# A decoder layer on one core: 18 of the 22 gate and up pairs of each SwiGLU as seven block products of 256 columns

## The reference

```
x = x + 0.5 * swiglu(rms_norm(x, g1), Wg1, Wu1, Wd1)     # d_ff 2816
x = x + mixer(rms_norm(x, g2))                           # pooling and windowed attention
x = x + 0.5 * swiglu(rms_norm(x, g3), Wg2, Wu2, Wd2)
x = x + sigmoid(rms_norm(x, g4) @ Wg) * (p @ Wp)
swiglu(h, Wg, Wu, Wd) = (silu(h @ Wg) * (h @ Wu)) @ Wd
```

## Time and profile before

| | |
|---|---|
| median of 3 runs | 924.93 us |
| profiled execution, first to last instruction (its span) | 923.8 us |
| TensorE busy, matmuls | 918.1 us, 4166 matmuls |
| VectorE / ScalarE / GpSimd busy | 300.1 / 337.4 / 408.1 us |
| granted TensorE clock | full speed throughout |

### The profile page before, as it was taken

How to read it: one execution, slowest core, us unless ns; L and a number is a source line. 1 busy time by engine, 2 the same in 40 slices (tenths; PEclk the granted TensorE clock), 3 DMA queues, 4 the chain that set the end, 5 groups by cost and what they waited for, 6 DMA issues and landing times.

```text
span 923.8 us, 11585 instructions
## 1 busy us (share of the span) xinstructions
PE 918.1 (99%) x4166; PEld 758.7 (82%) x4166; DVE 300.1 (32%) x479; ACT 337.4 (37%) x499; POOL 408.1 (44%) x192
## 2 busy tenths in 40 slices
PE   9999999999999999999999999999999999999998
PEld 8888888888888888887788888888888888888887
DVE  7522121111200501778958621112222200400552
ACT  5633232223321411568844632233322321321451
POOL 0544444444444444256665444444444444444430
PEclk9999999999999999999999999999999999999999
DMA  7633333333223243221224243333333323232211
GB/s 213 176 114 91 94 110 91 91 93 109 93 92 92 90 114 92 69 71 55 70 70 115 75 129 91 91 101 104 91 91 99 105 92 91 95 111 91 92 66 49
DMA packets 131044, 89.28 MB, mean 97 GB/s; under 512 B 11552, under 2 KB 116296, under 8 KB 131016
## 3 DMA queue, kind: packets, MB, share of 16 engines
q1 hardware_dynamic: 131000, 88.90, 32.7%
q10 hardware_dynamic: 16, 0.00, 0.0%
HBM read 86.80 MB, written 2.10 MB: 96 GB/s over the span
## 4 chain that ended last, share of the span: by engine, by line
PE 98%; DVE 1%; ACT 0%; issue 0%; DVEq 0%
PE bank L1282 32%; PE bank L1283 31%; PE bank L1284 31%; PE bank L1297 1%; PE bank L1507 1%; PE bank L1370 0%; DVE pr_lo L1093 0%; PE bank L1406 0%; ACT probs L623 0%; DVE d_lo L1054 0%; DVE probs L1086 0%; DVE probs L1071 0%; PE bank L1462 0%; PE bank L1463 0%; ACT w_hi L450 0%
## 5 line engine op out<-in xcount | busy, mean ns | idle before, releaser
L350 POOL TENSOR_TENSOR w_lo<-raw,w_hi 128x1024 fp32r<-128x1024 f32 x157 | 382.0, 2435 | 473.2 <-ACT w_hi L450 250.0
L1282 PE MATMUL bank<-h_hi,w_hi 128*128 128x512 f32 x844 | 329.9, 391 | 0.0
L1284 PE MATMUL bank<-h_hi,w_lo 128*128 128x512 f32 x844 | 328.6, 389 | 0.0
L1283 PE MATMUL bank<-h_lo,w_hi 128*128 128x512 f32 x844 | 328.5, 389 | 0.0
L1282 PEld LDWEIGHTS bank<-h_hi,w_hi 128*128 128x128 f32 x844 | 158.4, 188 | 33.9 <-issue 0.3
L1284 PEld LDWEIGHTS bank<-h_hi,w_lo 128*128 128x128 f32 x844 | 158.4, 188 | 32.9
L1283 PEld LDWEIGHTS bank<-h_lo,w_hi 128*128 128x128 f32 x844 | 158.5, 188 | 32.5
L508 ACT ACTIVATE w_hi<-raw 128x1024 fp32r<-128x1024 f32 x80 | 84.6, 1060 | 243.3 <-PE bank L1284 243.3
L450 ACT ACTIVATE w_hi<-raw 128x1024 fp32r<-128x1024 f32 x77 | 81.4, 1059 | 221.4 <-PE bank L1284 221.4
L1282 PE MATMUL bank<-act_hi,w_hi 128*128 (+1 forms) x352 | 136.9, 389 | 0.0
L1283 PE MATMUL bank<-act_lo,w_hi 128*128 (+1 forms) x352 | 136.9, 389 | 0.0
(11 more groups left out here) (181 smaller groups left out, 593.8 us busy)
## 6 DMA issues: line engine op xcount, KB each, us to landing
raw<-in_ffn_w_down SPq DMA_DIRECT2D x44, 512.0 KB, 3.7
raw<-in_ffn_w_gate SPq DMA_DIRECT2D x42, 512.0 KB, 3.9
raw<-in_ffn_w_up SPq DMA_DIRECT2D x42, 512.0 KB, 3.9
raw<-in_w_ple_gate SPq DMA_DIRECT2D x8, 512.0 KB, 3.7
raw<-in_w_in SPq DMA_DIRECT2D x6, 512.0 KB, 4.0
raw<-in_w_in SPq DMA_DIRECT2D x8, 256.0 KB, 3.6
raw<-in_w_out SPq DMA_DIRECT2D x4, 512.0 KB, 3.5
raw<-in_w_out SPq DMA_DIRECT2D x8, 256.0 KB, 4.2
```

The costliest lines, as they stand in the source:

```text
L350: pool.tensor_tensor(w_lo[:, slot, :], raw[:, slot, :], f32(w_hi[:, slot, :]), ALU.subtract).then_inc(w_ready, 1)
L1282: nc.tensor.matmul(dst, a_hi, b_hi, start=first, stop=False)
L1283: nc.tensor.matmul(dst, a_hi, b_lo, start=False, stop=False)
L1284: return nc.tensor.matmul(dst, a_lo, b_hi, start=False, stop=last)
```

## The change

Tiles 4 to 21 of each SwiGLU (18 of 22, `FAST`) are no longer 2 chunks x 24 matmuls of 512 columns. Gate and up weight blocks are seen as a 2 x 2 block matrix (input channels 0 to 511 and 512 to 1023, gate and up), h as a 2 x 2 block matrix (the same channels, tokens 0 to 255 and 256 to 511). Seven products of sums of blocks replace eight products of blocks. Each of the seven is 4 steps x 3 matmuls of 256 columns, so a tile has 84 of these. Tiles 0 to 3 stay as they were.

In this text p1 to p7 are the seven products in TensorE's order. p1 and p2 start c1 (PSUM) and c3; p3 is added to c1; p4 starts c2; p5 is added to c1, p6 to c3, p7 to c1. Between them ScalarE copies c1 after p1, c3 after p2 and c1 after p3 to SBUF (`keep`), and VectorE adds these copies to c2 after p4, c1 after p5 and c3 after p6 (`combine`). TensorE waits for the first copy ahead of p3, the third ahead of p5, and the second addition ahead of p7, which overwrites c1's sum.

- New for each tile: VectorE forms four 512-column sums of weight blocks from `raw` (`sums`) and the lo of the up chunk (`u_rest`); ScalarE rounds the gate half, both 1024-column sums and the up chunk; GpSimd writes the lo of the gate half (512 columns) and of both sums (1024 each). All of it is done one tile ahead.
- Activations stay in float32 (`act_f`) and are split to hi and lo chunk by chunk in the down projection (`act_split` on ScalarE, `act_rest` on VectorE).
- New for each SwiGLU, beside tiles 0 to 3: h times gain in float32 (8 instructions, ScalarE), four block differences of it (VectorE), their hi and lo; -rstd is kept in a PSUM bank.
- p's load, transposes, rounding and rests move from the opening to the end of the second SwiGLU's down projection.

```diff
+    PLAIN = 4
+    FAST = NF - PLAIN
+    WH = CHUNK // 2
+    TH = S // 2
...
+            act_f = sb("act_f", [P, NF, S], stack=phase)
+            wx_hi = sb("wx_hi", [P, 3, CHUNK], F32R, stack=phase)
+            wx_lo = sb("wx_lo", [P, 3, CHUNK], F32R, stack=phase)
+            xs_hi = sb("xs_hi", [P, 3, HALF, TH], F32R, stack=phase)
+            xs_lo = sb("xs_lo", [P, 3, HALF, TH], F32R, stack=phase)
+            sa = sb("sa", [P, CHUNK], stack=phase)
...
+        sb_f = tmp[:, 2:4, :].rearrange("p a c -> p (a c)")
+        neg_gate = tmp[:, 0, :]
+        up_1, kept_7 = tmp[:, 1, 0:TH], tmp[:, 1, TH:S]
+        kept_1, kept_61 = sumsq[:, 0:TH], sumsq[:, TH:S]
...
+            def fast_lo(n, c0):
+                with pool.Fori(2, QUADS) as quad:
+                    for p in range(2):
+                        f = quad * 2 + p
+                        m = f + n * FAST - PLAIN
+                        pool.wait_ge(g_hi, m + 1)
+                        pool.tensor_tensor(wx_lo[:, 2, g_cols(p)], raw[:, raw_g(c0, p), WH:],
+                                           f32(wx_hi[:, 2, g_cols(p)]), ALU.subtract)
+                        pool.wait_ge(sa_hi, m + 1)
+                        pool.tensor_tensor(lo_at(sa_slot(c0, p)), sa[:], f32(hi_at(sa_slot(c0, p))),
+                                           ALU.subtract).then_inc(w_ready, 1)
+                        pool.wait_ge(w_hi_done, f * 2 + c0 + 2)
+                        pool.wait_ge(u_ready, m + 1)
+                        pool.tensor_tensor(lo_at(sb_slot(c0, p)), sb_f, f32(hi_at(sb_slot(c0, p))),
+                                           ALU.subtract).then_inc(w_ready, 1)
+            for slot in range(SLOTS):
+                lo_of(slot, FFN1 + SLOTS + slot + 1)
+            fast_lo(0, FFN1)
...
+                split(c0 + SLOTS + 1)
+                silu(n, 0, tmp[:, 0, :])
+                for d in range(HALF):
+                    h_gained(n, d)
+                split(c0 + SLOTS + 2)
+                for d in range(HALF, KD):
+                    h_gained(n, d)
+                split(c0 + SLOTS + 3)
+                silu(n, 1, tmp[:, 1, :])
+                x_round(n, 0)
+                x_round(n, 1)
+                silu(n, 2, tmp[:, 0, :])
+                x_round(n, 2)
+                if n == 0:
+                    act.wait_ge(gain_ready, 3)
+                nc.scalar.activation(bank[4 * (1 - n) + 3][:], rstd[:], ACT.Copy, scale=-1.0)\
+                    .then_inc(neg_ready, 1)
+                g_round(n, c0, 2, 0)
+                sa_round(n, c0, 2, 0)
+                u_round(n, c0, 2, 0)
+                sb_round(n, c0, 2, 0)
+                silu(n, 3, tmp[:, 1, :])
+                act.wait_ge(w_used, c0 + 2 * PLAIN)
+                act.wait_ge(act_made, n * NF + PLAIN)
+                x_round(n, 3)
+                def pair(q, p, following):
+                    keep(n, q, p, 0)
+                    if following:
+                        g_round(n, c0, *following)
+                        sa_round(n, c0, *following)
+                    else:
+                        act_split(n, c0, 0, 0)
+                    keep(n, q, p, 1)
+                    keep(n, q, p, 2)
+                    if following:
+                        u_round(n, c0, *following)
+                        sb_round(n, c0, *following)
+                    else:
+                        act.wait_ge(w_used, c0 + GU - 2)
+                        split(c0 + GU)
+                        act_split(n, c0, 1, 1)
+                    silu(n, q * 2 + p, neg_gate)
...
+                def sums(q, p):
+                    f = q * 2 + p
+                    m = f + n * FAST - PLAIN
+                    g, u = raw[:, raw_g(c0, p), :], raw[:, raw_u(c0, p), :]
+                    dve.wait_ge(raw_loaded[raw_u(c0, p)], loads_of(raw_u(c0, p), c0 + 2 * p + 1, q))
+                    dve.wait_ge(w_ready, f * 2 + c0 - 1)
+                    dve.wait_ge(raw_loaded[raw_g(c0, p)], loads_of(raw_g(c0, p), c0 + 2 * p, q))
+                    nc.vector.tensor_tensor(sa[:, 0:WH], g[:, WH:], g[:, 0:WH], ALU.add).then_inc(s_made, 1)
+                    nc.vector.tensor_tensor(sa[:, WH:], u[:, 0:WH], g[:, 0:WH], ALU.add).then_inc(s_made, 1)
+                    dve.wait_ge(w_ready, f * 2 + c0)
+                    dve.wait_ge(s_made, m * 4 + 1)
+                    nc.vector.tensor_tensor(sb_f[:, 0:WH], sa[:, 0:WH], u[:, 0:WH], ALU.add).then_inc(s_made, 1)
+                    dve.wait_ge(s_made, m * 4 + 3)
+                    nc.vector.tensor_tensor(sb_f[:, WH:], sb_f[:, 0:WH], u[:, WH:], ALU.add).then_inc(s_made, 1)
+                def u_rest(q, p):
+                    dve.wait_ge(u_hi, q * 2 + p + n * FAST - PLAIN + 1)
+                    nc.vector.tensor_tensor(lo_at(u_slot(c0, p)), raw[:, raw_u(c0, p), :], f32(hi_at(u_slot(c0, p))),
+                                            ALU.subtract).then_inc(u_ready, 1)
+                def combine(q, p, i):
+                    m = q * 2 + p + n * FAST - PLAIN
+                    dst, src, old, have = ((up_1, bank[4 * n + 2], kept_1, 1),
+                                           (neg_gate[:, TH:S], bank[4 * n + 3 * p], kept_7, 2),
+                                           (neg_gate[:, 0:TH], bank[4 * n + 1], kept_61, 3))[i]
+                    dve.wait_ge(part_done, m * 6 + i + 4)
+                    dve.wait_ge(kept, m * 3 + have)
+                    nc.vector.tensor_tensor(dst, src[:, 0:TH], old, ALU.add).then_inc(c_made, 1)
+                def fast_gate(q, p):
+                    f = q * 2 + p
+                    dve.wait_ge(c_made, (f + n * FAST - PLAIN) * 3 + 3)
+                    dve.wait_ge(neg_ready, n + 1)
+                    nc.vector.tensor_tensor(neg_gate, neg_gate, bank[4 * (1 - n) + 3][:], ALU.mult)\
+                        .then_inc(gate_scaled, 1)
+                def fast_up(q, p):
+                    f = q * 2 + p
+                    dve.wait_ge(silu_done, f + n * NF + 1)
+                    nc.vector.tensor_tensor(act_f[:, f, 0:TH], up_1, neg_gate[:, 0:TH], ALU.mult)
+                    dve.wait_ge(w_used, f * 2 + c0 + 2)
+                    nc.vector.tensor_tensor(act_f[:, f, TH:S], bank[4 * n + 3 * p][:, 0:TH], neg_gate[:, TH:S],
+                                            ALU.mult).then_inc(act_made, 1)
...
+                plain_gate(0)
+                plain_up(0)
+                plain_gate(1)
+                dve.wait_ge(hf_made, KD * n + HALF)
+                nc.vector.tensor_tensor(x1_f, hf[0][:, :, 0:TH], hf[0][:, :, TH:S], ALU.subtract).then_inc(x_diff, 1)
+                plain_up(1)
+                dve.wait_ge(hf_made, KD * n + KD)
+                nc.vector.tensor_tensor(x3_f, hf[1][:, :, TH:S], hf[0][:, :, TH:S], ALU.subtract).then_inc(x_diff, 1)
+                dve.wait_ge(x_diff, 4 * n + 1)
+                nc.vector.scalar_tensor_tensor(x2_f, x1_f, -1.0, hf[1][:, :, TH:S], ALU.mult, ALU.subtract)\
+                    .then_inc(x_diff, 1)
+                dve.wait_ge(x_diff, 4 * n + 3)
+                nc.vector.scalar_tensor_tensor(x4_f, x2_f, -1.0, hf[1][:, :, 0:TH], ALU.mult, ALU.subtract)\
+                    .then_inc(x_diff, 1)
+                x_rest(0)
+                plain_gate(2)
+                x_rest(1)
+                x_rest(2)
+                plain_up(2)
+                sums(2, 0)
+                u_rest(2, 0)
+                plain_gate(3)
+                plain_up(3)
+                x_rest(3)
+                def pair(q, p, following):
+                    if following:
+                        sums(*following)
+                    else:
+                        act_rest(0, 0)
+                        dve.wait_ge(act_made, (n + 1) * NF - 1)
+                    combine(q, p, 0)
+                    if following:
+                        u_rest(*following)
+                    combine(q, p, 1)
+                    combine(q, p, 2)
+                    fast_gate(q, p)
+                    if not following:
+                        act_rest(1, 1)
+                    fast_up(q, p)
...
+                h11, h21 = ((h_hi[:, k:k + HALF, 0:TH], h_lo[:, k:k + HALF, 0:TH]) for k in (0, HALF))
+                h22 = h_hi[:, HALF:KD, TH:S], h_lo[:, HALF:KD, TH:S]
+                x1 = h_hi[:, 0:HALF, TH:S], h_lo[:, 0:HALF, TH:S]
+                x3, x2, x4 = ((xs_hi[:, i, :, :], xs_lo[:, i, :, :]) for i in range(3))
+                def pair(quad, p):
+                    f = quad * 2 + p
+                    m = f + n * FAST - PLAIN
+                    c1, c2, c3 = bank[4 * n + 3 * p], bank[4 * n + 2], bank[4 * n + 1]
+                    w11, w12 = halves_of(u_slot(c0, p))
+                    s1, s3 = halves_of(sa_slot(c0, p))
+                    s2, s4 = halves_of(sb_slot(c0, p))
+                    w22 = wx_hi[:, 2, g_cols(p)], wx_lo[:, 2, g_cols(p)]
+                    pe.wait_ge(act_made, f + n * NF - 1)
+                    pe.wait_ge(u_ready, m + 1)
```

(94 more changed lines are left out.)

220 lines of the change are left out of this document (130 added, 90 removed).

## The result

The changed kernel took 929.25 us (median of 4 runs, 926.78 to 931.99) against 924.90: ratio 1.0047, 95% interval 1.0028 to 1.0066. On another chip it was 928.94 us (6 runs, 927.08 to 931.31) against 925.03: 1.0038, interval 1.0025 to 1.0051. It is slower, by about 0.4%, and it spreads over 5 us where the kernel before stays within about 1 us (one of its 11 runs on that second chip, 926.94 us, apart). I had forecast 917.6.

What follows compares the result with a forecast made beforehand. TensorE, busy 918.1 of 923.8 us, was taken as the bound. 923.8 - 31.7 (matmuls) + 10.2 (port) + 13.7 (entry) + 0.5 (opening) = 916.5, with 1.1 to the median 917.6 us; own range 908 to 927, wide 902 to 936.

Steps and rivals of the forecast that it cites:

- The two signs of being wrong: TensorE's idle time standing elsewhere, above all on `gate_scaled` or GpSimd's rests, or a matmul distance other than 0.119 us.
- "Cost 0" (part 4): Down projection: the added ScalarE, VectorE and GpSimd work is covered by TensorE's 5.44 us a chunk, costing 0.
- TensorE's own work: All 36 fast tiles: 84 matmuls at 0.119 us replace 48 at 0.227, 10.88 to 10.0 us a tile, -31.7 us.
- The port: Fast tiles: VectorE and GpSimd contend for their shared port, 0 to 0.8 us a tile, 0.3 taken, +10.2 us.
- the two orders: Fast tiles: GpSimd's gate rest gets the port after VectorE's sum 3 (no cost) or before it (p7 0.8 us late).
- the deciding pair: Fast tiles: starts of VectorE's sum 3 and GpSimd's gate rest, 0.12 us apart, settle the port order.
- The entry: Preparation before and in tile 4 of both SwiGLUs makes TensorE wait: +13.7 us, between +7 and +18.
- The opening: Kernel's start: moving p's transposes out wins only 0.3 of 0.8 us, as the statistics matmul waits for VectorE: +0.5 us.
- The clock: Rival, chance 0.05: TensorE idling in the entry drops to half clock, +5 to +15 us, 927 at the middle.
- The base: Whole kernel: summed from the profiled span of 923.8 us, with 1.1 us added to reach the median of the runs.
- wide range of 902 to 936: Whole kernel time: covers the better half of the order-holds case and the lost order with its price.
- the rivals: Port order holds, about 905 us (0.22); port order lost, 934.6 us (0.28); clock falls in the entry, 927 (0.05).

Runs made afterwards that it cites:

- the swap on GpSimd: Changed kernel with GpSimd writing the rest of the first weight sum before the rest of the gate half: 913.11 us, ratio 0.9877 to the kernel before.

## Why the prediction was wrong

The mechanism of the steady state and of the entry was right; a stage that I had put at zero was not, and that turned the sign: with its order mended the kernel takes 921.96 us against 925.03. The two signs of being wrong that I had named both came: idle time of TensorE stood elsewhere (on `act_rest`, 4.9 us), and the distance was not 0.119 us.

- **The down projection, "Cost 0" (part 4): this step failed.** I compared totals (3.5 of 5.44 us in the port) and checked each chunk, but not the boundary of the halves, where ScalarE's old work for x stands between two splits. Measured: +2.6 and +3.0 us in the profiled run (3.9 less p's 0.85), and 1.6 and 1.35 us more where the clock fell behind it. With the order swapped both go: 7.0 us. This step alone is more than the loss against the kernel before.
- **TensorE's own work, mis-sized.** 0.120 us a matmul, not 0.119: 36 x (10.88 - 10.08) = 28.8 us won, not 31.7. I had read 11 distances and named the 3 us as the price of 1 ns. (Seven products for eight leave out an eighth of the columns, 12.5%, not "a seventh".)
- **The port.** Forecast 0 to 0.8 us a tile, 0.3 taken, with the two orders alternating; they do, and the deciding pair is the one I named. All of what is left of the gate and up stages is 28.8 + 0.3 - 5.3 - 10.5 (entry) = 13.3 us, of which 10.1 are p7's waits; forecast 10.2. The other 3.2 were in no term: behind each wait the second matmul starts another 0.1 us late (23 times), and the half-clock stretch in tile 4 took 1.5 us, less the 0.7 us by which this run's opening was faster. That the order and not the load costs this, the swap on GpSimd shows.
- **The entry.** Forecast 13.7 us; the waits sum to 3.61 + 0.50 + 1.96 in the first and 1.63 + 0.49 + 1.95 + 0.39 in the second SwiGLU, 10.5. Places and order were right.
- **The opening.** Forecast +0.5: the statistics matmul starts 0.65 us later than its turn, so of the 0.8 us of p's transposes only 0.1 is won, and not 0.3.
- **The clock.** I gave it 0.05 and placed it in the entry. It falls there in both profiled runs of the changed kernel and costs nothing in the end: where it fell behind p5's wait and made tile 4 longer, p7 then waited 0.51 us in every second tile, against 0.66 in the other profile, and the stage took the same 190.5 us; at the boundary it falls in one of them and costs 1.6 and 1.35 us. Such falls can make the 2.5 us between the profiled run (granted clock 0.997) and the median (0.994), but no run at the median was profiled.
- **The base.** Every run of both kernels whose span is known lies 1.7 to 1.8 us over it. The 1.1 us that I added came from setting one run's span beside another's median; 0.7 us.

From 917.6: +0.7 (base) + 5.6 (boundary) + 2.9 (matmul) - 3.2 (entry) + 3.1 (tiles) = 926.7, and the profiled run took 926.8. These terms were read from that run, so the sum only shows that none is missing. That the entry (3.2 too much) and the tiles (3.1 too little) cancel is luck. The median of 929.25 lies outside the forecast's own 908 to 927 and inside the wide range of 902 to 936, which the rivals had opened.

## What to carry to other kernels

Two engines that share a port are here served by who asks first, and a difference of 0.06 us between their requests was worth 0.6 to 0.9 us in every second tile: give the long instruction a producer that it must wait for, so that the burst of short ones is always through. When a conversion moves into another stage, read that stage's seams and not its average, above all where a queue holds older work between two things that the bound engine needs. And a change that looks lost by 0.4% may be two changes of order from a gain of 2%.
